# The final sum of a mixture-of-experts encoder: every tile's rows added by TensorE instead of every second tile's

## The chip, the core and the metric

The kernel runs on one core of one Trainium2 chip. The metric is the device time of one execution in microseconds (us). The kernel before was run three times: median 1764.89 us, lowest 1763.58, highest 1769.98.

## The reference

The reference is one layer of a bidirectional encoder trunk on 1024 tokens of 1024 float32 values: an input projection, three mixers (Hyena, RWKV7 in both directions, 2D neighbourhood attention), an output projection, and a hierarchical mixture of experts of which each token uses two. The change concerns its last lines. There each token gets the two rows that its experts computed, weighted with its two gates, added to its residual row x, and then a root mean square norm over its 1024 values with the weights norm_f_g:

```python
        x = x + hier_moe(h, moe_wg[l], moe_bg[l], moe_we[l], moe_be[l],
                         moe_w1[l], moe_w3[l], moe_w2[l]).reshape(Bn, L, D_MODEL)
    return rmsnorm(x, norm_f_g)

def rmsnorm(x, g):
    x32 = x.astype(jnp.float32)
    y = x32 * lax.rsqrt(jnp.mean(x32 * x32, axis=-1, keepdims=True) + NORM_EPS)
    return y.astype(x.dtype) * g
```

## The kernel before

The program is a row of blocks: the front (projection and filters), the mixers, the RWKV scan, the output projection with the router, the experts, and at the very end `combine` (line 2718), the only function that the change touches. Inside a block each engine works through its own list in program order, and semaphores set what waits for what; nothing is reordered by a planner.

When `combine` starts, the residual rows x of the 1024 tokens lie in SBUF as eight tiles of 128 tokens (`S.x2[:, t, :]`, 128 partitions by 1024 values, `NT` is 8). The expert rows lie in HBM (`S.ys`), and `S.place` holds for each token where its two rows are; `S.gate` holds its two gates. The work is per tile t:

- POOL (line 2751) issues two indirect DMAs, which gather the tile's two sets of expert rows into `ya[t][0]` and `ya[t][1]`. All sixteen are issued one behind the other; each tile has a semaphore `y_in[t]`, full at 32.
- For the even tiles ScalarE first makes two diagonal matrices of 128x128 from the identity, with the gates on the diagonal (line 2795, four tiles, eight activations, ahead of all else on its list). TensorE waits for them and for the gather and adds in PSUM: for each half of 512 columns identity times x (line 2762), then each diagonal times its gathered rows (line 2764). `acc` is four tensors of two PSUM banks each, one for each even tile, so all eight banks are in use. `acc_full` counts.
- For the odd tiles VectorE adds in SBUF: two operations rows * gate + x over 1024 columns (line 2774), each with a drain (line 2776) behind it; `summed` counts.
- ScalarE squares the sum over the 1024 columns with an accumulated output (line 2805), VectorE turns that into mean plus epsilon (line 2783), ScalarE takes the root (line 2807), VectorE the reciprocal (line 2785), and VectorE scales the tile with it and with norm_f_g into `S.x2` (line 2788). ScalarE and VectorE do this in the order of the tiles, 0 to 7.
- SP (line 2744) stores each scaled tile, one DMA of 512 KB, and waits for all stores at the end.

VectorE's list is: the adds of tile 1, the statistics and scaling of tiles 0 and 1, the adds of tile 3, tiles 2 and 3, and so on. On TensorE only even tiles stand, in order, each with its identity and diagonal matmuls after the two waits. In front of `combine` stands a block for experts with more tokens than one block holds (line 2643), in which nothing is done in these runs; its end is where the engines of `combine` start.

Of the kernel before, what the change touches and what calls it, by code (L numbers as in the profile page):

```python
# [17 lines left out]
ALU = mybir.AluOpType  # L18
ACT = mybir.ActivationFunctionType
# [7 lines left out]
NT = L // P  # L27
HALF = 512
# [2689 lines left out]
def combine(nc, A, S, sem, out):  # L2718

    ctx = ExitStack()
    with ctx:
        sb = lambda n, s, t=F32: ctx.enter_context(nc.sbuf_tensor(n, s, t))
        ps = lambda n, s: ctx.enter_context(nc.psum_tensor(n, s, F32))
        gb = S.proj[:, 8, :]
        ya = [[S.proj[:, 9 + 2 * t + k, :] for k in range(2)] for t in range(NT)]
        junk = S.proj[:, 25, :]
        ss, rs = sb("z_ss", [P, NT]), sb("z_rs", [P, NT])
        diag = sb("z_diag", [P, NT, 2, P])  # L2730
        acc = [ps(f"z_acc{j}", [P, 2, HALF]) for j in range(NT // 2)]
        on_pe = lambda t: t % 2 == 0
        par_in, stored = sem("z_par_in"), sem("z_stored")
        y_in = [sem(f"z_y_in{t}", True) for t in range(NT)]
        summed, squares, mean_ready, root_ready, normed = (sem("z_summed"), sem("z_squares"), sem("z_mean"),
                                                           sem("z_root"), sem("z_normed"))
        diag_ready, acc_full = sem("z_diag_ready"), sem("z_acc_full")
        with nc.Block() as block:
            @block.sync
            def _(e):  # L2740
                e.dma_start(gb, A["norm_f_g"].to_broadcast([P, D])).then_inc(par_in, 16)
                for t in range(NT):
                    e.wait_ge(normed, t + 1)
                    e.dma_start(out[TILE_ORDER[t] * P:(TILE_ORDER[t] + 1) * P, :], S.x2[:, t, :]).then_inc(stored, 16)
                e.wait_ge(stored, 16 * NT)

            @block.gpsimd
            def _(e):
                for t in range(NT):
                    for k in range(2):  # L2750
                        e.indirect_dma_start(ya[t][k], None, S.ys.rearrange("b p d -> (b p) d"),  # L2751
                                             bass.IndirectOffsetOnAxis(ap=S.place[:, t, k:k + 1], axis=0)
                                             ).then_inc(y_in[t], 16)

            @block.tensor
            def _(e):
                for t in range(0, NT, 2):
                    e.wait_ge(diag_ready, t // 2 + 1)
                    e.wait_ge(y_in[t], 32)
                    for h in range(2):  # L2760
                        cut = slice(h * HALF, (h + 1) * HALF)
                        e.matmul(acc[t // 2][:, h, :], S.ident[:, :], S.x2[:, t, cut], start=True, stop=False)  # L2762
                        for k in range(2):
                            m = e.matmul(acc[t // 2][:, h, :], diag[:, t, k, :], ya[t][k][:, cut], start=False, stop=(k == 1))  # L2764
                    m.then_inc(acc_full, 1)

            @block.vector
            def _(e):
                e.wait_ge(par_in, 16)

                def add(t):
                    e.wait_ge(y_in[t], 32)
                    for k in range(2):
                        e.scalar_tensor_tensor(out=S.x2[:, t, :], in0=ya[t][k], scalar=S.gate[:, t, k:k + 1],  # L2774
                                               in1=S.x2[:, t, :], op0=ALU.mult, op1=ALU.add)
                        e.drain()  # L2776
                    e.sem_inc(summed, 1)

                for t in range(NT):
                    if on_pe(t):  # L2780
                        add(t + 1)
                    e.wait_ge(squares, t + 1)
                    e.tensor_scalar(rs[:, t:t + 1], ss[:, t:t + 1], 1.0 / D, EPS, ALU.mult, ALU.add).then_inc(mean_ready, 1)  # L2783
                    e.wait_ge(root_ready, t + 1)
                    e.reciprocal(rs[:, t:t + 1], rs[:, t:t + 1])  # L2785
                    e.drain()  # L2786
                    whole = acc[t // 2][:, :, :].rearrange("p h c -> p (h c)") if on_pe(t) else S.x2[:, t, :]
                    e.scalar_tensor_tensor(out=S.x2[:, t, :], in0=whole, scalar=rs[:, t:t + 1], in1=gb,  # L2788
                                           op0=ALU.mult, op1=ALU.mult).then_inc(normed, 1)

            @block.scalar
            def _(e):
                for t in range(0, NT, 2):
                    for k in range(2):
                        m = e.activation(diag[:, t, k, :], S.ident[:, :], ACT.Copy, scale=S.gate[:, t, k:k + 1])
                    m.then_inc(diag_ready, 1)
                for t in range(NT):
                    if on_pe(t):
                        e.wait_ge(acc_full, t // 2 + 1)
                        whole = acc[t // 2][:, :, :].rearrange("p h c -> p (h c)")  # L2800
                    else:
                        e.wait_ge(summed, t // 2 + 1)
                        whole = S.x2[:, t, :]
                    e.drain()  # L2804
                    e.activation(junk, whole, ACT.Square, accum_out=ss[:, t:t + 1]).then_inc(squares, 1)  # L2805
                    e.wait_ge(mean_ready, t + 1)
                    e.activation(rs[:, t:t + 1], rs[:, t:t + 1], ACT.Sqrt).then_inc(root_ready, 1)  # L2807

# [24 lines left out]
def program(nc, A, out):  # L2833
    ctx = ExitStack()
    with ctx:
# [48 lines left out]
        with semaphores(nc, ctx, S) as sem:  # L2884
            combine(nc, A, S, sem, out)
# [98 lines left out]
```

## Time and profile before

| | |
|---|---|
| median of three runs | 1764.89 us (1763.58 to 1769.98) |
| the profiled execution's own time | 1765.18 us |
| its span in the profile | 1763.0 us |
| mean granted clock of TensorE | 0.96 |
| busy: TensorE / VectorE / ScalarE / POOL | 1628.1 / 1144.1 / 806.5 / 260.7 us |
| the stretch of `combine` | about 1718 to 1763 us of the span |

Each engine's busy time is summed over its instructions and says nothing of what waits for what. The chain of waits (the chain of work that ended last, followed back from the last instruction) says that. "Idle before" is how long an engine stood still ahead of an instruction, and the arrow what ended it. PEclk is the clock that was granted to TensorE: 1.00 is 2.4 GHz, 0.50 is 1.2 GHz. A float32 matmul call appears as two records; the ends of matmul records are modelled, so that records overlap, and the starts are what to read.

### The profile page before, as it was taken

The numbers are of one execution on the slowest core, as the hardware profiler recorded it, in microseconds if no ns is written. First come the engines' busy times: TensorE is split into PE (matmuls) and PEld (weight loads), VectorE is DVE, ScalarE is ACT, GpSimd is POOL, SyncE is SP. The second block draws the span as 40 slices with busy tenths as digits, with TensorE's granted clock in tenths as the row PEclk, the third lists the DMA queues.
The fourth block names the chain that finished last, engine by engine and source line by source line (L and its number), as shares of the span: only waits on it lengthen the run. The fifth ranks groups of instructions, "written<-read, shape, count | busy, mean of one in ns | idle before, by whom it ended". The sixth has DMA issues, their size and how long they took to land. (4 is left out here: it accounts for less than half of the span.)

```text
span 1763.0 us, 44528 instructions
## 1 busy us (share of the span) xinstructions
PE 1628.1 (92%) x18962; PEld 1238.0 (70%) x18962; DVE 1144.1 (65%) x1987; ACT 806.5 (46%) x1267; POOL 260.7 (15%) x287
## 2 busy tenths in 40 slices
PE   5999999998889779999977995999999999999985
PEld 4677777786564579999976885766776776677662
DVE  5558888865676546666756665666666666566755
ACT  5337666532232234554543112654555555565543
POOL 0020000001000234545530000100100010010003
PEclk8999999999999899999998996999999999999997
DMA  5214545434225236556553247799999999999927
GB/s 176 84 73 118 150 112 160 115 101 191 72 75 214 80 116 197 165 181 196 164 166 116 72 156 286 295 388 377 378 389 388 371 385 390 372 382 388 381 84 298
DMA packets 159445, 387.98 MB, mean 220 GB/s; under 512 B 67719, under 2 KB 115207, under 8 KB 144872
## 3 DMA queue, kind: packets, MB, share of 16 engines
q1 hardware_dynamic: 146664, 340.39, 53.1%
q0 software_dynamic: 8064, 29.36, 4.2%
q10 hardware_dynamic: 4608, 16.78, 2.3%
q8 instruction: 67, 1.10, 0.2%
q14 instruction: 42, 0.34, 0.1%
HBM read 294.75 MB, written 56.10 MB: 199 GB/s over the span
## 5 line engine op out<-in xcount | busy, mean ns | idle before, releaser
L2485 DVE TENSOR_TENSOR e_rl<-proj,e_rh 128x1024 fp32r<-128x1024 f32 x256 | 306.8, 1223 | 115.0 <-ACT e_rh L2422 114.2
L2422 ACT ACTIVATE e_rh<-proj 128x1024 fp32r<-128x1024 f32 x256 | 263.7, 1057 | 69.2 <-PE e_ph L52 48.3
L2403 PE MATMUL e_py<-mix,proj 128*128 128x512 f32 x512 | 225.0, 592 | 0.7 <-issue 0.7
L52 PE MATMUL e_ph<-e_rh,e_xh 128*128 128x512 f32 x512 | 219.1, 428 | 2.8 <-DVE e_xl L2492 2.6
L52 PE MATMUL e_ph<-e_rh,e_xl 128*128 128x512 f32 x512 | 201.3, 393 | 0.0
L52 PE MATMUL e_ph<-e_rl,e_xh 128*128 128x512 f32 x512 | 200.1, 391 | 0.0
L52 PE MATMUL a_b<-a_xh,a_wh 128*128 128x512 f32 x432 | 177.6, 411 | 5.9 <-DVE a_wl L592 3.4
L2403 PEld LDWEIGHTS e_py<-mix,proj 128*128 128x128 f32 x512 | 97.0, 190 | 110.7 <-issue 108.1
L52 PE MATMUL a_b<-a_xh,a_wl 128*128 128x512 f32 x432 | 169.9, 393 | 0.0
L52 PE MATMUL a_b<-a_xl,a_wh 128*128 128x512 f32 x432 | 169.7, 393 | 0.0
L52 PEld LDWEIGHTS e_ph<-e_rh,e_xh 128*128 128x128 f32 x512 | 97.1, 190 | 28.3 <-issue 8.4
L52 PEld LDWEIGHTS e_ph<-e_rl,e_xh 128*128 128x128 f32 x512 | 96.9, 189 | 24.8 <-issue 7.4
L1828 ACT ACTIVATE s_th<-s_lv 128x512 f32<-128x512 f32 x128 | 69.8, 598 | 96.2 <-PE s_lv L1590 86.2
L52 PEld LDWEIGHTS a_b<-a_xh,a_wh 128*128 128x128 f32 x432 | 82.1, 190 | 43.7 <-issue 22.2
L52 PEld LDWEIGHTS e_ph<-e_rh,e_xl 128*128 128x128 f32 x512 | 96.4, 188 | 21.5
L1712 DVE TENSOR_TENSOR s_xx<-s_lv,s_eyes 128x256 f32<-128x256 f32 x160 | 63.2, 419 | 49.6 <-PE s_lv L1570 41.7
L52 PEld LDWEIGHTS a_b<-a_xl,a_wh 128*128 128x128 f32 x432 | 82.1, 190 | 18.1 <-issue 2.2
L52 PEld LDWEIGHTS a_b<-a_xh,a_wl 128*128 128x128 f32 x432 | 81.9, 190 | 17.9
L2461 ACT ACTIVATE e_yo<-e_py 128x512 f32<-128x512 f32 x32 | 19.2, 601 | 156.8 <-PE e_py L2403 156.8
L2618 DVE COPY e_yo<-e_py 128x512 f32<-128x512 f32 x32 | 22.1, 692 | 97.2 <-PE e_py L2403 97.2
L1884 POOL TENSOR_TENSOR s_al<-proj 128x512 f32<-128x512 f32 x64 | 80.0, 1287 | 0.0
L2354 POOL COPY idx<-ids 128x1 uint32<-128x1 uint32 x30 | 5.5, 184 | 490.2 <-ACTq L2426 490.2
(396 smaller groups left out, 3313.4 us busy)
## 6 DMA issues: line engine op xcount, KB each, us to landing
proj<-in_moe_w SPq DMA_DIRECT2D x64, 2048.0 KB, 15.0
mix<-in_moe_w SPq DMA_DIRECT2D x32, 2048.0 KB, 8.3
proj<-scan_operands SPq DMA_DIRECT2D x64, 320.0 KB, 4.0
expert_rows<-e_yo ACTq DMA_DIRECT2D x32, 512.0 KB, 11.0
proj<-in_w_in SPq DMA_DIRECT2D x27, 512.0 KB, 4.2
proj<-proj SPq DMA_DIRECT2D x16, 768.0 KB, 4.0
s_rec<-proj SPq DMA_DIRECT2D x16, 768.0 KB, 5.4
scan_operands<-late SPq DMA_DIRECT2D x40, 256.0 KB, 2.6
```

The costliest lines, as they stand in the source:

```text
L52: m = e.matmul(out, lhs[a], rhs[b], start=first and n == 0, stop=last and n == 2)
L1712: e.tensor_tensor(xx[:, g, :, :, :].rearrange("p b q c -> p b (q c)"), lv[g][:, :, 0:2 * CH], eyes[:, :, :].rearrange("p (b q) c -> p b (q ...
L1828: e.activation(th[:, g, :, :, :, :].rearrange("p b k q c -> p b (k q c)"), both[g], ACT.Copy).then_inc(th_kept, 1)
L1884: e.tensor_tensor(al[:, l - 1, :, :], ab, bcast(level[:, l, :], 2 * HU), ALU.mult).then_inc(al_ready, 1)
L2354: e.tensor_copy(idx[j][:, :], S.ids[:, ds(b, 1)]).then_inc(idx_ready, 1)
L2403: m = e.matmul(py[h][:, :], at[:, k, :], w2[j][:, k, h * HALF:(h + 1) * HALF], start=(k == 0), stop=(k == KF - 1))
L2422: e.activation(rh[s % RING][:, :], piece(j, s), ACT.Copy).then_inc(high, 1)
L2461: e.activation(yo[j][:, 0:HALF], py[0][:, :], ACT.Copy).then_inc(y_kept, 1)
L2485: e.tensor_tensor(rl[s % RING][:, :], piece(j, s), rh[s % RING][:, :].bitcast(F32), ALU.subtract).then_inc(low, 1)
L2618: e.tensor_copy(yo[j][:, HALF:D], py[1][:, :]).then_inc(y_kept, 1)
```

## The change

TensorE now adds all eight tiles. The four pairs of PSUM banks are taken in turn: tile t uses `acc[t % 4]`, and from tile 4 on TensorE first waits until the tile four before it has been scaled (`normed`). A tile's four matmul calls with the diagonals come after the waits for the diagonals and the gather as before, while its two identity calls now stand ahead of these waits. VectorE's `add` and the semaphore `summed` are gone; what is left to it is the statistics and the scaling, always out of PSUM. ScalarE makes the diagonals of all eight tiles at the start and squares always out of PSUM.

```diff
         acc = [ps(f"z_acc{j}", [P, 2, HALF]) for j in range(NT // 2)]
-        on_pe = lambda t: t % 2 == 0
+        bank = lambda t: acc[t % len(acc)]
+        whole = lambda t: bank(t)[:, :, :].rearrange("p h c -> p (h c)")
...
             @block.tensor
             def _(e):
-                for t in range(0, NT, 2):
-                    e.wait_ge(diag_ready, t // 2 + 1)
+                for t in range(NT):
+                    if t >= len(acc):
+                        e.wait_ge(normed, t - len(acc) + 1)
+                    for h in range(2):
+                        e.matmul(bank(t)[:, h, :], S.ident[:, :], S.x2[:, t, h * HALF:(h + 1) * HALF], start=True, stop=False)
+                    e.wait_ge(diag_ready, t + 1)
                     e.wait_ge(y_in[t], 32)
                     for h in range(2):
-                        cut = slice(h * HALF, (h + 1) * HALF)
-                        e.matmul(acc[t // 2][:, h, :], S.ident[:, :], S.x2[:, t, cut], start=True, stop=False)
                         for k in range(2):
-                            m = e.matmul(acc[t // 2][:, h, :], diag[:, t, k, :], ya[t][k][:, cut], start=False, stop=(k == 1))
+                            m = e.matmul(bank(t)[:, h, :], diag[:, t, k, :], ya[t][k][:, h * HALF:(h + 1) * HALF],
+                                         start=False, stop=(k == 1))
                     m.then_inc(acc_full, 1)
 
             @block.vector
             def _(e):
                 e.wait_ge(par_in, 16)
 
-                def add(t):
-                    e.wait_ge(y_in[t], 32)
-                    for k in range(2):
-                        e.scalar_tensor_tensor(out=S.x2[:, t, :], in0=ya[t][k], scalar=S.gate[:, t, k:k + 1],
-                                               in1=S.x2[:, t, :], op0=ALU.mult, op1=ALU.add)
-                        e.drain()
-                    e.sem_inc(summed, 1)
-
                 for t in range(NT):
-                    if on_pe(t):
-                        add(t + 1)
                     e.wait_ge(squares, t + 1)
                     e.tensor_scalar(rs[:, t:t + 1], ss[:, t:t + 1], 1.0 / D, EPS, ALU.mult, ALU.add).then_inc(mean_ready, 1)
                     e.wait_ge(root_ready, t + 1)
                     e.reciprocal(rs[:, t:t + 1], rs[:, t:t + 1])
                     e.drain()
-                    whole = acc[t // 2][:, :, :].rearrange("p h c -> p (h c)") if on_pe(t) else S.x2[:, t, :]
-                    e.scalar_tensor_tensor(out=S.x2[:, t, :], in0=whole, scalar=rs[:, t:t + 1], in1=gb,
+                    e.scalar_tensor_tensor(out=S.x2[:, t, :], in0=whole(t), scalar=rs[:, t:t + 1], in1=gb,
                                            op0=ALU.mult, op1=ALU.mult).then_inc(normed, 1)
 
             @block.scalar
             def _(e):
-                for t in range(0, NT, 2):
+                for t in range(NT):
                     for k in range(2):
                         m = e.activation(diag[:, t, k, :], S.ident[:, :], ACT.Copy, scale=S.gate[:, t, k:k + 1])
                     m.then_inc(diag_ready, 1)
                 for t in range(NT):
-                    if on_pe(t):
-                        e.wait_ge(acc_full, t // 2 + 1)
-                        whole = acc[t // 2][:, :, :].rearrange("p h c -> p (h c)")
-                    else:
-                        e.wait_ge(summed, t // 2 + 1)
-                        whole = S.x2[:, t, :]
-                    e.drain()
-                    e.activation(junk, whole, ACT.Square, accum_out=ss[:, t:t + 1]).then_inc(squares, 1)
+                    e.wait_ge(acc_full, t + 1)
+                    e.drain()
+                    e.activation(junk, whole(t), ACT.Square, accum_out=ss[:, t:t + 1]).then_inc(squares, 1)
```

## Rows read from the trace of the kernel before

**Rows 1.** Chain of waits, 1716 to 1738: start us, us, what.

```profile
1720.17 6.20 DMA proj<-expert_rows,place
...
1726.50 2.05 PE z_acc L2762 x2
...
1734.53 1.11 ACT proj L2805 x2
...
1735.66 1.28 ACT L2807
```

**Rows 2.** VectorE's timeline: start us, us, engine, line, operation, out<-in, count.

```profile
1746.96 2.64 DVE L2774 SCALAR_TENSOR_TENSOR proj<-proj,gate 128x1024 f32<-128x1024 f32 x2
1749.72 0.15 DVE L2783 TENSOR_SCALAR z_rs<-z_ss 128x1 f32<-128x1 f32 x1
...
1756.19 0.15 DVE L2783 TENSOR_SCALAR z_rs<-z_ss 128x1 f32<-128x1 f32 x1
...
1756.85 1.28 DVE L2788 SCALAR_TENSOR_TENSOR proj<-z_acc,z_rs,proj 128x1024 f32<-128x1024 f32 x1
...
1758.70 1.28 DVE L2788 SCALAR_TENSOR_TENSOR proj<-proj,z_rs 128x1024 f32<-128x1024 f32 x1
```

**Rows 3.** TensorE's timeline in the final sum, same columns.

```profile
1726.50 2.05 PE L2762 MATMUL z_acc<-proj,ident 128*128 128x512 f32 x2 [10.26 <-DMA proj<-expert_rows,place]
...
1731.69 1.02 PE L2762 MATMUL z_acc<-proj,ident 128*128 128x512 f32 x2
...
1734.27 1.02 PE L2762 MATMUL z_acc<-proj,ident 128*128 128x512 f32 x2
...
1739.42 1.02 PE L2762 MATMUL z_acc<-proj,ident 128*128 128x512 f32 x2
...
1748.00 1.88 PE L2764 MATMUL z_acc<-proj,z_diag 128*128 128x512 f32 x4
```

**Rows 4.** Groups by line, 1717 to 1763: busy us, mean ns, idle before.

```profile
L2764 PE MATMUL z_acc<-proj,z_diag 128*128 128x512 f32 x32 | 16.7, 647 | 0.0
...
L2774 DVE SCALAR_TENSOR_TENSOR proj<-proj,gate 128x1024 f32<-128x1024 f32 x8 | 10.3, 1282 | 12.8 <-DMA proj<-expert_rows,place 12.5
L2762 PE MATMUL z_acc<-proj,ident 128*128 128x512 f32 x16 | 9.2, 659 | 10.3 <-DMA proj<-expert_rows,place 10.3
...
L2795 ACT ACTIVATE z_diag<-ident,gate 128x128 f32<-128x128 f32 x8 | 2.4, 387 | 4.8 <-PEq L2643 4.8
```

**Rows 5.** Windows: stretch, length, busy by engine, PEclk, DMA share, GB/s.

```profile
1716.24:1718.00 1.76, 0.00 (x1) 0.00 (x0) 0.17 (x1) 0.00 (x0) 0.00 (x0) 0.99 0.00 0
1718.00:1726.00 8.00, 0.00 (x0) 0.00 (x0) 0.00 (x0) 2.44 (x8) 5.55 (x6) 0.50 0.76 245
1726.50:1731.50 5.00, 5.00 (x6) 2.16 (x7) 2.44 (x2) 0.00 (x0) 3.78 (x5) 0.50 1.01 407
1731.70:1752.00 20.30, 18.18 (x43) 7.79 (x41) 12.85 (x21) 9.30 (x19) 5.45 (x6) 1.00 0.83 334
1752.20:1763.00 10.80, 0.00 (x0) 0.00 (x0) 6.88 (x9) 2.51 (x6) 0.00 (x0) 0.50 0.48 194
```

**Rows 6.** POOL's timeline, first and last of sixteen gathers; line L2751's DMAs to landing.

```profile
1718.93 0.94 POOL L2751 DMA_INDIRECT proj<-expert_rows,place  x1 [76.16 <-POOLq L2643]
...
1737.73 0.94 POOL L2751 DMA_INDIRECT proj<-expert_rows,place  x1 [0.30 <-issue]
...
DMA to landing us min/median/max: 5.0/6.4/8.0
```

**Rows 7.** SP's stores, line L2744: issue to landing.

```profile
DMA to landing us min/median/max: 2.6/2.6/6.5
```

**Rows 8.** TensorE's timeline in the experts: neighbouring float32r records.

```profile
1701.65 0.39 PE L52 MATMUL e_ph<-e_rh,e_xl 128*128 128x512 f32 x1
1701.88 0.39 PE L52 MATMUL e_ph<-e_rh,e_xh 128*128 128x512 f32 x1
```

More of the change, by code:

```diff
@@ L2731, in combine @@
         acc = [ps(f"z_acc{j}", [P, 2, HALF]) for j in range(NT // 2)]
-        on_pe = lambda t: t % 2 == 0
+        bank = lambda t: acc[t % len(acc)]
+        whole = lambda t: bank(t)[:, :, :].rearrange("p h c -> p (h c)")
         par_in, stored = sem("z_par_in"), sem("z_stored")
         y_in = [sem(f"z_y_in{t}", True) for t in range(NT)]
-        summed, squares, mean_ready, root_ready, normed = (sem("z_summed"), sem("z_squares"), sem("z_mean"),
-                                                           sem("z_root"), sem("z_normed"))
+        squares, mean_ready, root_ready, normed = sem("z_squares"), sem("z_mean"), sem("z_root"), sem("z_normed")
         diag_ready, acc_full = sem("z_diag_ready"), sem("z_acc_full")
```

## The prediction

> **What bounds the kernel now.** I read the chain of waits from its end first, because the change touches the last 45 us only. The chain enters the final sum with the first gathered rows, which land at 1726.37 of the span (the DMA piece of 6.20 us from 1720.17), goes through TensorE to 1734.48 and then to ScalarE [rows 1]. From 1737.4 on it runs, with short hops to ScalarE, on VectorE to the end. VectorE's timeline shows why: two tiles take one period of 6.47 us, from the short operation at 1749.72 to the one at 1756.19 [rows 2], made of two 1.28 us adds for the odd tile (2.64 us with their overlap, and drains beside them) and two scalings of 1.28 us with their statistics. The last scaling ends at 1758.70 + 1.28 = 1759.98 [rows 2]; the span ends at 1763.0, so 3.02 us lie behind it: the store, which lands 2.6 us after its issue in the median [rows 7], and the end of the block.
>
> TensorE's own timeline [rows 3] shows what this engine pays. A float32 call of 128x512 is two records: the present code makes 8 identity and 16 diagonal calls, and the trace has 16 and 32 records [rows 4]. The group at 1726.50 is half a tile (2 identity records, 4 diagonal); the next half starts at 1731.69, so six records take 5.19 us, 0.865 each. From there half a tile takes 1734.27 - 1731.69 = 2.58 us, and a tile 1739.42 - 1734.27 = 5.15 us, 0.43 a record. The first pace goes with a granted clock of 0.50 (1.2 GHz), the second with 1.00 (2.4 GHz) [rows 5]. So TensorE needs 5.15 us for an even tile and VectorE 6.47 us for a pair: today VectorE decides, by a small margin, and TensorE is done about 10 us before the span's last scaling (its last group starts at 1748.00 [rows 3]).
>
> **The change part by part.**
>
> VectorE loses eight adds of 1.282 us, 10.3 us in all [rows 4], with their drains and their waits for the gathers. What is left per tile is the mean, the reciprocal and the scaling: from 1756.19 to 1756.85 + 1.28 = 1758.13, or 1.94 us [rows 2], the two hops to ScalarE included. ScalarE's square and readout are 1.11 us [rows 1]. Neither engine can be the pace at that price.
>
> TensorE gets four more tiles, 48 more records. The odd tiles' rows were added beside its work; now they stand in the same queue. At the full clock a tile is 12 x 0.43 = 5.15 us, so a pair costs 10.3 us where VectorE's period was 6.47. That is the whole of my case: the sum moves from an engine that takes 2.64 us a tile to one that takes 5.15, and the latter becomes the bound.
>
> The identity matmuls now stand ahead of the waits for the diagonals and the gathers. This takes work off the path for tile 0 alone, since in every later tile TensorE is already late and never idles. Its four identity records can run from about 1718.2, when the block's other engines start; at the low clock that is 4 x 0.865 = 3.5 us, to 1721.7, hidden under the gather that lands at 1726.37 [rows 1]. Were that cover gone they would cost these 3.5 us. Left for tile 0 are 8 diagonal records from 1726.50. With the clock as now, six run at the low one until 1731.69 and two at the full one: 5.19 + 0.86 = 6.05 us, ending at 1732.55. The bounds are 8 x 0.43 = 3.43 us and 8 x 0.865 = 6.92 us; I take 6.05, because the granted clock was 0.50 from 1718 to 1731.5 [rows 5] and fell within 1.8 us of TensorE's going quiet at 1716.24; the new quiet stretch, 1721.7 to 1726.5, is longer.
>
> Then seven tiles follow without a gap: 7 x 5.15 = 36.05 us, to 1768.60. ScalarE started 0.26 us after TensorE's tile ended (1734.27 [rows 3] to 1734.53 [rows 1]), its square and readout are 1.11 us [rows 1] with 0.03 to VectorE's start, VectorE's part 1.94 us: the last scaling ends at 1768.60 + 0.26 + 1.14 + 1.94 = 1771.94. The 3.02 us behind it I keep. Today the store before the last starts 1.85 us ahead of it and takes 2.6 [rows 7], so at most 0.75 us of overlap could go; the other end is nothing. Span 1774.96, or 11.96 us more.
>
> Small edits cost nothing, and this is what hides them. The diagonals double from 8 to 16 ScalarE activations; eight took 2.44 us from 1718.25, so sixteen end near 1723.1, 3.3 us before TensorE needs the first; with that cover gone they would cost 2.4 us. The new wait of TensorE for the scaling of the tile four before it is met long ahead: tile 0 is scaled 0.26 + 1.14 + 1.28 + 1.94 = 4.6 us after its sum is full (1.28 is the table load of [rows 1]), while TensorE comes back to its banks 15 us after. Behind that wait stand all of TensorE's later matmuls, so it would hurt at once if it bound. The odd tiles' gather waits move from VectorE to TensorE. The sixteenth gather is issued at 1737.73 and a gather lands 8.0 us after issue at most [rows 6], so by 1745.7; tile 7's diagonals want it near 1765.1. POOL's queue issues the same sixteen gathers in the same order. SP's queue holds one store a tile behind the scaling, now 5.15 us apart and not 1.9 or 4.6, so none waits for another.
>
> **The sum.** Removed: VectorE's path from 1734.5 to 1760.0. Put in: TensorE's to 1768.6 and one tile's tail. Net +11.96 us on the profiled execution's span; with its own time of 1765.18 us that is 1777.1, and against the median of 1764.89, which is 0.3 lower, 1776.9 us. That is 0.68% slower. I count 0.5%, 8.8 us, as what a measurement of this kernel can tell from no change; the line lies at 1773.7 us.
>
> **The rivals.**
>
> *The clock is full when the gathers land.* The early identities could raise or hold it. Tile 0's eight records would then take 3.43 us in place of 6.05: 2.6 us less, 1774.3 us. For it: TensorE works 3.5 us at a stretch that was empty before. Against it: after the last records (end near 1749.9) the granted clock of 1.00 lasted to about 1752, and was 0.50 from 1752.2 on [rows 5]; the new kernel's quiet stretch of 4.8 us is longer than both pauses before a fall that the rows show. 13 in 100.
>
> *The identities are nearly free, so not slower.* This is the one that ends on the other side. Its place is each tile's four identity records, which in the new order stand together with the same stationary operand. If the array took them at the pace that float32r records show, 0.23 us from 1701.65 to 1701.88 [rows 8], a tile would take 8 x 0.43 + 4 x 0.23 = 4.36 us and the end would come 7 x 0.79 = 5.5 us earlier, at 1771.4, within 0.5%. If they cost nothing, a tile is 3.43 us and the seven save 12.0 us: a tie at 1764.9. It decides from a tile time under 4.69 us (8.8 us for the 0.5%: 3.2 us off seven tiles). Against it: a record takes 0.43 us in identity and diagonal groups alike, with another stationary operand before it, so the operand's reload is not what sets the pace. 5 in 100.
>
> *The clock falls between tiles.* If TensorE ran at the low clock throughout, its 8 + 84 records of 0.865 us would take 79.6 us from 1726.50 in place of 6.05 + 36.05 = 42.1, which is 37.5 us more than forecast, 1814.4 us; a fall for one tile alone costs 5.2 us. Against it: in the present kernel the granted clock stays 1.00 from 1731.7 to 1752 with TensorE busy without a gap in its matmuls [rows 5], and the new queue has no wait that is open when TensorE reaches it. 4 in 100.
> The Trainium skill warns of just that ("TensorE: Matmul & The Clock Gate", section "A second HAM failure mode: psum-queue depth-cycling"): a kernel that cycled through PSUM banks had small pauses between its matmul groups, and its clock kept falling and rising. By that rule this change, which takes the bank pairs in turn, would run partly at the low clock and give a time in between 1777 and 1814 us. The trace of before, which also passes through four bank pairs, shows one rise and no such fall, so I go by the rows.
>
> **How the numbers follow.** Forecast 72 in 100, the rivals 13, 5 and 4, and 6 for things I can't name (a stall of TensorE's instruction supply would now count in full, where before it had 10 us of cover). The range must cover the forecast and the first rival with the scatter of the runs shown (1763.58 to 1769.98): 1774.3 less 2 gives 1772.0 at the low end, and above, the 0.87 us of an all-low tile 0 and some 3 us of scatter give 1781.0. Slower by over 0.5%: nearly all of the forecast, two thirds of the first rival, the third, and half of the unnamed, 82 in 100. Within 0.5%: 15, from the first and second rivals and scatter. Faster: 3.
>
> **What would show it.** Right: the chain of waits stays on TensorE from 1726.5 to about 1768.6; its timeline shows tiles 5.15 us apart; four identity records near 1718 to 1722; VectorE idles some 3.2 us a tile for ScalarE, which waits for TensorE; the eight stores come 5.15 us apart. The first rival shows as a granted clock of 1.00 at 1726.5, the second as tiles under 4.7 us apart, the third as 0.50 in stretches after 1732. The forecast is wrong if the chain still runs on VectorE, or if tile 7's matmuls end before 1765.

## The result and the profile after

The changed kernel took 1778.34 us (median of four runs, 1776.59 to 1779.55), the kernel before in the same comparison 1765.28 us. The ratio is 1.0068 with a 95% interval of [1.0051, 1.0085]: slower by 0.68%, as forecast (1776.9 us), and inside the range of 1772 to 1781 us. The profiled execution's own time is 1776.59 us, its span 1774.6 us. That span is 11.6 us over the one before; the final sum is measured better from the first gather's issue on POOL to the end of the span, since the blocks ahead of it end at another moment in each execution. This stretch, called the tail below, was 1763.0 - 1718.93 = 44.07 us before and is 1774.6 - 1718.49 = 56.11 us now: 12.04 us more.

The chain of waits of the changed kernel, from 1716 to the end (start us, us, what), answers to [rows 1]:

```profile
1719.73 6.27 DMA proj<-expert_rows,place
1726.00 0.14 issue
1726.13 6.16 PE z_acc L2766 x8
1732.29 1.72 PE z_acc L2761 x4
1734.01 3.43 PE z_acc L2766 x8
...
1763.19 1.72 PE z_acc L2761 x4
1764.91 3.45 PE z_acc L2766 x8
...
1768.43 1.12 ACT proj L2792 x2
...
1770.24 1.28 DVE proj L2780
```

Once the gather has landed, the chain is on TensorE alone for 42 us, and passes through ScalarE and VectorE only for the last tile. There is no wait between the groups. TensorE's timeline, to be read beside [rows 3], gives the pace by its starts:

```profile
1717.83 3.48 PE L2761 MATMUL z_acc<-proj,ident 128*128 128x512 f32 x4 [2.00 <-PEq L2643]
1726.13 6.16 PE L2766 MATMUL z_acc<-proj,z_diag 128*128 128x512 f32 x8 [4.83 <-DMA proj<-expert_rows,place]
1732.13 1.88 PE L2761 MATMUL z_acc<-proj,ident 128*128 128x512 f32 x4
...
1737.28 1.88 PE L2761 MATMUL z_acc<-proj,ident 128*128 128x512 f32 x4
...
1764.74 3.60 PE L2766 MATMUL z_acc<-proj,z_diag 128*128 128x512 f32 x8
```

Tile 0's identities ran at 1717.83, in the shadow of the gather. Its eight diagonal records took 1732.13 - 1726.13 = 6.00 us, and a tile takes 1737.28 - 1732.13 = 5.15 us. Who waits for whom in the tail (us in total, times, longest) shows the other engines:

```profile
DVE z_rs L2776 <- ACT proj L2792: 38.9, 8, 17.6
ACT proj L2792 <- PE z_acc L2766: 34.0, 8, 9.8
```

VectorE stands still for 38.9 us behind ScalarE, which stands still for 34.0 us behind TensorE. The adds' group of [rows 4] is gone, and TensorE has 64 and 32 records in place of 32 and 16:

```profile
L2766 PE MATMUL z_acc<-proj,z_diag 128*128 128x512 f32 x64 | 31.3, 636 | 4.8 <-DMA proj<-expert_rows,place 4.8
L2761 PE MATMUL z_acc<-proj,ident 128*128 128x512 f32 x32 | 16.6, 646 | 2.0 <-PEq L2643 2.0
```

The clock by windows (columns as in [rows 5]):

```profile
1721.00:1724.00 3.00, 0.31 (x1) 0.00 (x0) 0.00 (x0) 1.59 (x6) 2.39 (x3) 1.00 0.92 305
1724.50:1726.00 1.50, 0.00 (x0) 0.00 (x0) 0.00 (x0) 0.00 (x0) 0.98 (x2) 0.50 0.97 385
1726.13:1731.00 4.87, 4.87 (x6) 2.17 (x7) 0.00 (x0) 0.00 (x0) 3.65 (x5) 0.50 1.02 407
1731.70:1768.00 36.30, 36.30 (x86) 15.96 (x84) 11.21 (x21) 10.51 (x22) 4.88 (x6) 1.00 0.54 217
```

The granted clock did rise during the early identities, to 1.00 by 1721, but TensorE then had nothing to do, and before the gather landed the clock was back at 0.50.

### The profile page after: what moved, and what is told of

Same layout as the page of the kernel before. It is cut to its first block and busy times, and to the rows that moved or that the text cites. A ratio compares the mean times of both kernels' runs of the same rounds, so it can differ in the third digit from the quotient of the medians.

```text
span 1774.6 us, 44620 instructions
## 1 busy us (share of the span) xinstructions
PE 1650.2 (93%) x19010; PEld 1247.0 (70%) x19010; DVE 1134.6 (64%) x1979; ACT 808.7 (46%) x1275; POOL 260.5 (15%) x287
```

## The experiments

Theory: TensorE's float32 records, 0.43 us each at the full clock and 12 a tile, are the bound; the clock adds some 2.6 us once, in tile 0. The rivals are those of the prediction: nearly free identities, a clock that is full at the start, a clock that falls between tiles. Each kernel below was profiled once, the changed kernel and `combined` twice; the tail is from that profile. The tail also holds two things that vary between executions of kernels with the same first tile: when the first gather lands (6.5 to 7.6 us after the first issue) and when the clock rises in tile 0. Steps of a microsecond are read with both beside them.

**Without the identities** (`no_identity`). The edit:

```diff
-                    for h in range(2):
-                        e.matmul(bank(t)[:, h, :], S.ident[:, :], S.x2[:, t, h * HALF:(h + 1) * HALF], start=True, stop=False)
...
-                                         start=False, stop=(k == 1))
+                                         start=(k == 0), stop=(k == 1))
```

> The changed kernel without its sixteen identity calls: x is left out of the final sum, all else as it was. Theory (TensorE's records are the bound, 0.43 us each at the full clock): a tile falls from 12 records and 5.15 us to 8 records and 3.43 us; tile 0 keeps its 8 diagonal records. The last scaling comes 7 x 1.72 = 12.0 us earlier than in the changed kernel, tail from the first gather's issue to the span's end 56.1 - 12.0 = 44.1 us, time near 1766 us, level with the kernel before. Rival (identity records are nearly free, the tile time comes from elsewhere, such as the diagonals' operand loads or the statistics): tiles stay near 5 us apart, tail over 54 us. Rival (the gathers or VectorE come next): tiles over 3.43 us apart, with TensorE's wait put down to a gather or to the scaling.

Measured: 1766.05 us, ratio to the kernel before 0.9994 [0.9979, 1.0008]; tail 1766.0 - 1721.91 = 44.09 us. The chain of waits of this kernel:

```profile
1729.07 30.71 PE z_acc L2764 x64
...
1759.85 1.12 ACT proj L2790 x2
```

64 records in 30.71 us, TensorE never waiting: the first tile almost wholly at the low clock (about 6.7 us), the others 3.43 us each. An identity record costs as much as a diagonal one, and sixteen calls (fourteen of them on the path) are the whole 12 us. The agreement to 0.02 us is luck: tile 0 took 0.7 us longer than in the changed kernel, and its gather landed 0.5 us sooner. The rival of cheap identities falls. So does the thought that gathers or VectorE stand right behind TensorE: even at 3.43 us a tile they don't bind.

**TensorE kept busy until the gather lands** (`filler`). The edit, behind the identities of tile 0:

```diff
+                    for n in range(5 if t == 0 else 0):
+                        e.matmul(bank(3)[:, n % 2, :], S.ident[:, :], S.x2[:, 3, 0:HALF], start=True, stop=True)
```

> The changed kernel with five more identity calls for TensorE right behind the two of tile 0, into the banks of tile 3, which tile 3 overwrites later. They fill the quiet stretch before the first gather lands, which in the changed kernel's profile was 4.8 us, with 10 records. Theory (tile 0 took 6.0 us because the granted clock fell to 0.50 in the quiet stretch): with TensorE busy the clock stays at 1.00, tile 0's 8 diagonal records take 3.43 us, the tail is 56.1 - 2.6 = 53.5 us and the time some 2.6 us under the changed kernel's. Rival (the low pace at the start has another reason, such as the gathers' writes into the memory that TensorE reads): the 8 records take 6 us still and the tail stays at 56.1 us. Rival (the fillers run over the gather's landing): tile 0 starts later than 0.2 us behind the landing.

Measured: 1774.32 us, ratio 1.0049 [1.0024, 1.0074]; tail 1770.7 - 1717.24 = 53.46 us. Two windows, the quiet stretch that is now filled and tile 0's diagonals:

```profile
1720.00:1724.50 4.50, 4.43 (x11) 1.69 (x9) 0.00 (x0) 1.34 (x5) 3.47 (x4) 1.00 0.95 312
1724.80:1728.30 3.50, 3.50 (x8) 1.59 (x9) 0.00 (x0) 0.00 (x0) 2.70 (x3) 1.00 1.02 412
```

All eight records ran at a granted clock of 1.00, in 3.5 us, with the DMA engines as full as before. So the slow start is the clock's, not the gathers', and it is worth 2.5 us, for the 2.6 us between the two cases of the prediction. Only the trace shows this: the intervals of the two ratios, this one and [1.0051, 1.0085], overlap.

**The identities behind the waits again** (`identity_behind`):

```diff
-                    for h in range(2):
-                        e.matmul(bank(t)[:, h, :], S.ident[:, :], S.x2[:, t, h * HALF:(h + 1) * HALF], start=True, stop=False)
                     e.wait_ge(diag_ready, t + 1)
                     e.wait_ge(y_in[t], 32)
+                    for h in range(2):
+                        e.matmul(bank(t)[:, h, :], S.ident[:, :], S.x2[:, t, h * HALF:(h + 1) * HALF], start=True, stop=False)
```

> The changed kernel with each tile's two identity calls put back behind the waits for the diagonals and the gather, as in the kernel before. Theory (the move hides tile 0's four identity records and nothing else): tile 0 has 12 records behind the landing, six at the low clock and six at the full one, 5.19 + 2.58 = 7.8 us in place of 6.0, the later tiles stay 5.15 us apart, the tail is 56.1 + 1.7 = 57.8 us. Rival (the early calls hide more, for instance a short pause at every tile's wait): over 0.3 us more per tile, tail over 59.5 us. Rival (the early calls change the clock): the rise to 1.00 comes at another distance from the first diagonal record, and the difference is 3.4 us if it comes at the end of the tile.

Measured: 1781.04 us, ratio 1.0083 [1.0059, 1.0106]; tail 1774.5 - 1716.87 = 57.63 us. In TensorE's timeline tile 0 begins at 1724.09 and tile 1 at 1732.03, 7.94 us later, and all later tiles are 5.15 us apart. The tails differ by 1.5 us, once and not in every tile. In tile 0 itself the move is worth 7.94 - 6.00 = 1.9 us; the gather landed 0.4 us sooner here than in the changed kernel (7.08 for 7.51 us after the first issue), which hides the rest.

**The kernel before with that move alone** (`ahead_alone`):

```diff
                 for t in range(0, NT, 2):
+                    for h in range(2):
+                        e.matmul(acc[t // 2][:, h, :], S.ident[:, :], S.x2[:, t, h * HALF:(h + 1) * HALF], start=True, stop=False)
                     e.wait_ge(diag_ready, t // 2 + 1)
                     e.wait_ge(y_in[t], 32)
                     for h in range(2):
                         cut = slice(h * HALF, (h + 1) * HALF)
-                        e.matmul(acc[t // 2][:, h, :], S.ident[:, :], S.x2[:, t, cut], start=True, stop=False)
```

> The kernel before with one part of the change alone: the identity calls of the four even tiles stand ahead of the waits, the odd tiles stay on VectorE. Theory (before, the end waits for VectorE, whose run of tiles starts when tile 0's sum is full): tile 0 is full 1.7 us earlier, VectorE's whole run with its period of 6.47 us moves forward by that, tail 44.1 - 1.7 = 42.4 us, time 1763.5 us, better than both kernels by a step that only the trace can show. Rival (something else releases VectorE's run, such as the odd tile's gathers or norm_f_g's load): no gain, tail 44.1 us. Rival (TensorE's sums become late for later tiles): VectorE's period grows beyond 6.47 us.

Measured: 1763.25 us, ratio 0.9985 [0.9967, 1.0003]; tail 1766.9 - 1725.61 = 41.29 us. VectorE's period stayed 6.47 us, and its run moved forward by 2.8 us and not 1.7. Its chain tells why:

```profile
1726.85 5.90 DMA proj<-expert_rows,place
...
1732.89 5.41 PE z_acc L2765 x8
```

The gather landed 0.3 us sooner after the first issue (7.14 us, before 7.44), and the clock rose sooner in tile 0, whose next tile starts at 1738.12, 5.23 us after 1732.89, where the forecast of the changed kernel had 6.05. These two make up the 1.1 us beyond the 1.7 expected of the move, and another execution need not repeat them. The useful half of the change is this half. The times alone do not show it, since the interval takes in 1. TensorE also waited 2.5 us for the gather of tile 6, which landed 27.1 us after the first issue; VectorE's work covered it.

**A share of the tiles in between** (`split_5_3`): tiles 0, 2, 4, 6 and 7 on TensorE.

```diff
-        on_pe = lambda t: t % 2 == 0
+        pe = [0, 2, 4, 6, 7]
+        on_pe = lambda t: t in pe
+        bank = lambda t: acc[pe.index(t) % len(acc)]
...
-                    if on_pe(t):
+                    if t + 1 < NT and not on_pe(t + 1):
                         add(t + 1)
```

> The kernel before with the identity calls ahead of the waits and five tiles (0, 2, 4, 6, 7) on TensorE, three (1, 3, 5) on VectorE. Theory (the end is the later of two queues, TensorE's 5.15 us a tile and VectorE's 1.9 us a scaling plus 2.7 us a pair of adds): TensorE is full 4 x 5.15 = 20.6 us after tile 0's sum, which is 12.5 to 13.6 us after the first gather's issue depending on when the clock rises, then 3.3 us of statistics and scaling and 3.0 to the end: tail 39.5 to 40.5 us. VectorE alone would allow the 41.3 us of the run with four tiles less one pair of adds, 38.6 us, so TensorE decides. Time 3.5 to 4.5 us under the kernel before. Rival (VectorE still decides): tail 38.6 us. Rival (every tile moved to TensorE costs as the whole change did, 12.0 / 4 = 3.0 us): tail 41.3 + 3.0 = 44.3 us.

Measured: tail 1758.0 - 1717.11 = 40.89 us, 0.4 over the expected; 1765.36 us, ratio 0.9998 [0.9986, 1.0011]. The fifth tile on TensorE cost nothing, though tile 0 was full 1.2 us later than in `ahead_alone` (13.7 us after the first issue, for 12.5); the three that remain then cost (56.11 - 40.89) / 3 = 5.1 us each, TensorE's full price of a tile, where the whole change looks like 3.0 us a tile over its four. The profile had something that was not expected, in ScalarE's timeline:

```profile
1735.31 0.20 ACT L2812 ACTIVATE z_rs<-z_rs 128x1 f32<-128x1 f32 x1 [0.42 <-issue]
1739.87 1.02 ACT L2810 ACTIVATE proj<-z_acc 128x1024 f32<-128x1024 f32 x1 [4.36 <-remote]
```

ScalarE stood still for 4.36 us with tile 2's sum ready since about 1735.9, and the profile cannot name the releaser. VectorE, late by this, then took the end of the chain; TensorE's queue alone (tile 0 full at 1730.77, then 20.6 and 6.4 us) would have given 40.7 us, so the stop cost this execution 0.2 us.

**The table load made early** (`ahead_preload`), on top of `ahead_alone`:

```diff
                     m.then_inc(diag_ready, 1)
+                e.activation(warm[:, 0:1], S.gate[:, 0, 0:1], ACT.Sqrt)
                 for t in range(NT):
```

> The kernel before with the identity calls ahead of the waits and one root of a gate behind the diagonals on ScalarE, written to a value nobody reads, so that the 1.28 us table load happens while the gathers are on their way. Theory (the load stands on the chain ahead of VectorE's run of tiles): tail 41.3 - 1.3 = 40.0 us, within 1.1 us for the clock's rise. Rival (a second load follows when squares and roots take turns): no gain or a loss of 1.28 us a tile.

Measured: tail 1763.2 - 1722.62 = 40.58 us; 1763.73 us, ratio 0.9990 [0.9977, 1.0004]. The load ran at 1724.40, behind the diagonals, and none followed. Tile 0's first statistic to its scaling fell from 1737.43 - 1735.67 = 1.76 us before to 0.66. Part was given back at a new place in the chain:

```profile
1742.52 11.04 DMA proj<-expert_rows,place
...
1753.58 1.28 DVE proj L2776
```

Tile 7's gather took 11.04 us and VectorE waited for it for 0.38 us.

**All of these together** (`combined`: five tiles on TensorE, identities ahead, fillers, early table load).

> Five tiles on TensorE and three on VectorE, the identity calls ahead, five filler calls in tile 0's wait so that the clock is full when the gathers land, and the table load made early. Theory (two queues): tile 0's sum is full 7.6 + 3.4 = 11.0 us after the first gather's issue, the last 20.6 us later, and 3.3 + 3.0 us follow: tail 38.0 us, 6 us under the kernel before (0.35%) and 18 us under the changed kernel. VectorE alone would allow 35.9 us. Rival (VectorE waits for the gathers of tiles 1, 3 and 5 and decides): tail over 39 us with VectorE on the chain to the end. Rival (the fillers run over the landing): tile 0 late, tail 38.5 us or more.

Measured: tail 1768.7 - 1726.70 = 42.0 us, where 38.0 was expected; 1764.60 us, ratio 0.9993 [0.9982, 1.0003]. A miss, and TensorE's timeline shows its place:

```profile
1748.08 1.88 PE L2764 MATMUL z_acc<-proj,ident 128*128 128x512 f32 x4
1751.89 5.37 PE L2772 MATMUL z_acc<-proj,z_diag 128*128 128x512 f32 x8 [1.94 <-DMA proj<-expert_rows,place]
1757.10 1.88 PE L2764 MATMUL z_acc<-proj,ident 128*128 128x512 f32 x4
```

Tile 6's diagonals start at 1751.89 where its identities end near 1749.8: 2.1 us of waiting for the gather, then 5.2 us for records that take 3.4. The clock was at 1.00 through the pause and fell about 0.9 us after TensorE had gone on (0.67 in the mean from 1752.0 to 1757.2). That is 3.9 of the 4.0 us. The kernel once more, unchanged (`combined_again`):

> The combined kernel once more, unchanged, for how well its tail repeats. If its miss (42.0 us for 38.0) belongs to the kernel, tile 6's gather lands 24.5 us or more after the first issue again and the tail is 41 to 43 us; if it was chance, the tail is 38 to 39 us.

Measured: tail 1763.9 - 1722.80 = 41.1 us, tile 6's gather at 1748.73 - 1722.80 = 25.9 us (25.1 the first time), and 2.69 us of waiting. The late gather repeats. The fall of the clock does not: after this longer pause the eight records took 3.5 us. The windows of tile 6, two of `combined` and then one of `combined_again`:

```profile
1751.90:1752.70 0.80, 0.80 (x2) 0.45 (x3) 0.65 (x2) 0.38 (x3) 0.00 (x0) 1.00 1.03 420
1752.90:1755.00 2.10, 2.10 (x4) 0.99 (x3) 2.03 (x3) 1.09 (x2) 0.00 (x0) 0.50 0.81 326
...
1748.90:1752.30 3.40, 3.40 (x8) 1.57 (x9) 2.71 (x6) 1.56 (x4) 0.00 (x0) 1.00 1.03 420
```

So of the 4.0 us only the wait, 2.1 and 2.9 us between the starts and ends of these groups, came back; what the clock added to it did not. ScalarE's stop does not repeat either: in `combined` it took tile 2 at 1749.40, some 6.5 us after TensorE had it; in `combined_again` within 0.3 us.

**The stores held back until the gathers are in** (`combined_hold`, and `split_5_3_hold` for the kernel with the share alone). One line on SP, ahead of the loop of stores:

```diff
+                e.wait_ge(y_in[NT - 1], 32)
```

> The combined kernel, with SP holding all stores until tile 7's gather has landed. In the combined kernel tile 6's gather landed 25.1 us after the first gather's issue, TensorE stood still for 1.9 us and ran tile 6 partly at the low clock; its tail was 42.0 us where 38.0 was expected. Theory (the stores of finished tiles take bandwidth from the gathers, whose DMA engines are full until then): without stores tile 6's gather lands by 23 us, TensorE does not wait for it, the clock stays at 1.00, tail 38 to 38.7 us. Rival (the gathers come late for another reason, such as their issue on POOL or the memory): tile 6's gather lands at 24.5 us or later again, tail 41 us or more. Rival (the held stores come too late themselves): the end waits for stores, over 3.3 us after the last scaling.

Measured: tail 1759.4 - 1719.51 = 39.89 us; 1762.25 us, ratio 0.9977 [0.9963, 0.9992]. The chain of this kernel:

```profile
1735.92 7.02 DMA proj<-expert_rows,place
1742.94 0.14 issue
1743.08 3.67 PE z_acc L2773 x8
...
1753.80 1.28 DVE proj L2797
```

Tile 6's gather landed 23.4 us after the first issue, in place of 25.1 and 25.9, TensorE waited 0.36 us and kept its clock (3.5 us for the eight records). Against this one profile the gather had lost 1.7 and 2.5 us beside the stores, and the amounts fit: until that landing SP's queue had moved 0.5 MB here, 1.6 and 1.8 MB in the other two. The hold has its price too: the last scaling ends at 1755.08 and the span 4.3 us later, not 3.0, which is the 1.3 us by which the tail misses the upper end expected. This version is faster than both kernels, by 0.23% against the one before (median 1767.26 us in that comparison).

> The kernel with five tiles on TensorE and three on VectorE, with all stores held until tile 7's gather has landed. Its tail without the hold was 40.9 us, with ScalarE standing still for 4.4 us at tile 2 (put down to an unknown queue), from 18.4 to 22.8 us after the first gather's issue. Theory A (that stop is a fetch of ScalarE's own that waits behind the full DMA engines, gathers above all): the hold shortens it little, under 1 us, since the gathers alone fill the engines until about 22 us; tail 39.5 to 41 us. Theory B (it is the stores): the stop goes, ScalarE takes tile 2 as soon as TensorE has it, tail 39.5 us or less.

Measured: tail 1761.9 - 1723.01 = 38.89 us; 1762.81 us, ratio 0.9983 [0.9970, 0.9997]. ScalarE's stop is absent, and the number is the one of theory B, but it does not settle it: tile 0 was full 11.9 us after the first issue here and 13.7 us in `split_5_3`, for the clock's rise and the gather's landing, and those 1.8 us are nearly all of the 2.0 us between the two tails. The granted clock was still 1.00 when the gather landed at 1729.54, and fell to 0.50 about 0.7 us later, under TensorE's records.

**The changed kernel once more** (`changed_again`):

> The changed kernel once more, unchanged. The theory of TensorE as the bound leaves only the clock's rise open: tiles 5.15 us apart as before, tile 0's eight diagonal records between 5.2 and 6.9 us, tail 55.3 to 57.0 us (56.1 the first time), wherever ScalarE or the gathers stand still. If other waits matter, the tail lies outside of that.

Measured: tail 1776.8 - 1720.69 = 56.11 us, the same as the first time; tiles 5.15 us apart, tile 0's diagonals 6.02 us.

## Why the prediction was right

**The bound.** The prediction moved the bound from VectorE's period of 6.47 us a pair to TensorE's 5.15 us a tile. Measured: 5.15 us between all tiles, no wait between them, two engines idle behind them; and without the identities the tail shrank by the price of their records, 12.02 us for 12.04 (in part by luck, as said there).

**Tile 0.** Forecast 6.05 us for its diagonals, measured 6.00 (6.02 again). The early identities ended near 1721.3 (forecast 1721.7). The clock rose to 1.00 during them, which the sum did not have; it was back at 0.50 some 3 us after they ended, within the quiet stretch of 4.8 us, so the comparison by which this rival got 13 in 100 held here, and `filler` shows what the rival would have brought. That the size came within 0.05 us is partly luck. With the same eight diagonal records behind the same early identities, tile 0 took 5.2 us in `ahead_alone` and `split_5_3_hold`, 5.4 in `ahead_preload` and 6.1 in `split_5_3`; without the identities it took 6.7. The clock followed no one course either: in `ahead_alone` the identities did not raise it at all, and in `split_5_3_hold` it was still 1.00 at the landing. The forecast took the one course that the rows of before had; its bounds of 3.43 and 6.92 us cover all of these.

**The last tile and the end.** Forecast 1.14 + 1.94 us from ScalarE's start to the last scaling's end, measured 1771.52 - 1768.43 = 3.09; 3.02 us behind it, measured 3.08. The tail was to grow by 11.96 us and grew by 12.04.

**What was costed at nothing.** The sixteen diagonals ended at 1722.6, 3.4 us ahead of the gather. TensorE's wait for a scaled tile never showed. The gathers landed within 8.6 us (9.7 again) and the stores stood 5.15 us apart. ScalarE's stop, which the prediction did not have and which five of the other kernels' profiles show, was covered: in `filler` ScalarE took tile 1 at 1737.17, 3.7 us after TensorE had it at 1733.45, and the tail was still the expected one.

**The rivals.** Cheap identities: refuted. The clock falling between tiles: it stayed at 1.00 from 1731.7 to 1768. The Trainium skill ("TensorE: Matmul & The Clock Gate", section "A second HAM failure mode: psum-queue depth-cycling") has small pauses between matmul groups behind that rival; this case's trace has no such pause and no fall in these 36 us, with four bank pairs taken in turn. The clock did fall under a later tile in `combined` and `ahead_alone`, after TensorE had waited 1.9 and 2.5 us for a gather, and did not after waits of 1.9 us in `ahead_preload` and 2.7 us in `combined_again`.

**What stays open.** What ScalarE waits for in those stops. It is not a fixed property of a kernel, since `combined` had it in one execution and not in the other, and in the five profiles that have it it ends 20 to 23 us after the first gather's issue. The DMA engines' mean busy share was 1.01 to 1.03 during the stop, and 1.01 to 1.04 in the microsecond after it, so their load alone does not say when it ends. That it is a fetch behind the gathers is a guess; no run isolates it.

## What to carry to other kernels

Before work is moved to an engine that looks idle, write both engines' cost of one unit beside each other: here two adds were 2.64 us on VectorE and the same sum 5.15 us on TensorE in float32, so the bound moved with the first extra tile and each one after it cost about 5 us. The split belongs where the two queues end together, and the cheap half of an edit (here the calls that need no late data, issued ahead of the wait) can be a gain alone where the whole is a loss. A step that hangs on the clock is worth a second profile before it is called a kernel's own. When the new bound is taken off, look at who shares the DMA engines: finished results going out can delay the inputs that the next tile waits for.

## What the runs showed that was not expected

- The same four identity records, 3.5 us at the low clock, were followed by a granted clock of 1.00 in the changed kernel (both profiles), `split_5_3` and `split_5_3_hold`, and of 0.50 until the gather landed in `ahead_alone` and `ahead_preload`.
- Waits of TensorE for a gather, of 1.9 us (`combined`) and 2.5 us (`ahead_alone`) by the profile, were followed by a fall of the clock that cost 1.8 us more; waits of 1.9 us (`ahead_preload`) and 2.7 us (`combined_again`) cost nothing more.
- With the stores of finished tiles beside it a gather landed about 2 us later: 25.1 and 25.9 us after the first issue with the stores, 23.4 in one profile without.
- ScalarE took a finished tile about 2 us (`no_identity`) to 6.5 us late (`combined`) while the DMA engines were full; of the two profiles of `combined` one shows it and one does not.
